# Gate sums of a recurrent stage by 64x64 blocks, and every second weight tile rounded by GpSimd

## The reference

```python
h = rmsnorm(x, norm_mix)
xr, gr, q, k, v, iq, ik, iw, ga, gb = split(h @ w_in)
# branch A, the recurrent one; D_RNN = 1024 channels in 16 blocks of 64
xc = causal_conv4(xr)
r = sigmoid(blockdiag(w_rg_a) @ xc + b_rg_a)       # 16 blocks of 64x64
i = sigmoid(blockdiag(w_rg_x) @ xc + b_rg_x)
log_a = 8 * r * log_sigmoid(lam)
a, u = exp(log_a), sqrt(-expm1(2 * log_a)) * (i * xc)
h_t = a_t * h_(t-1) + u_t                          # scan over the positions
branch_a = (h * gelu(gr)) @ w_rnn_out
# branch B: top-k by an indexer, then attention over the chosen keys with a position bias
branch_b = attend(q, k, v, iq, ik, iw) @ w_att_out
x += (sigmoid(ga) * branch_a + sigmoid(gb) * branch_b) @ w_o
x += swiglu(rmsnorm(x))
x += sigmoid(rmsnorm(x) @ w_ple_gate) * (p @ w_ple_proj)
y = rmsnorm(x)
```

## Time and profile before

| | us |
|---|---|
| median of 3 runs | 1044.59 (1043.33 to 1045.3) |
| the profiled execution, its own time | 1042.96 |
| its span in the profile | 1041.2 |
| PE busy | 1009.8 (97% of the span) |
| PEld (weight loads, beside PE) | 964.6 (93%) |
| DVE busy | 493.9 (47%) |
| ACT busy | 418.6 (40%) |
| POOL busy | 445.4 (43%) |

### The profile page before, as it was taken

How to read it: one execution, slowest core, us unless ns; L and a number is a source line. 1 busy time by engine, 2 the same in 40 slices (tenths; PEclk the granted TensorE clock), 3 DMA queues, 4 the chain that set the end, 5 groups by cost and what they waited for, 6 DMA issues and landing times.

```text
span 1041.2 us, 19261 instructions
## 1 busy us (share of the span) xinstructions
PE 1009.8 (97%) x7845; PEld 964.6 (93%) x7845; DVE 493.9 (47%) x769; ACT 418.6 (40%) x707; POOL 445.4 (43%) x301
## 2 busy tenths in 40 slices
PE   6999999999979999999999999999999999999997
PEld 4986998799978999899999999999999999999996
DVE  5127899588992534324364343333001333334474
ACT  5325234698983444323334322222112222233543
POOL 2424431367784444534542543343344334244530
PEclk9999999999999999999999999999999999999998
DMA  6733276452330443043253432322333322222502
GB/s 187 208 63 87 72 197 186 130 162 62 82 82 26 102 102 82 21 124 83 65 178 87 133 91 86 96 61 77 91 97 104 100 81 65 65 80 73 144 1 86
DMA packets 168751, 101.98 MB, mean 98 GB/s; under 512 B 12626, under 2 KB 160754, under 8 KB 168418
## 3 DMA queue, kind: packets, MB, share of 16 engines
q1 hardware_dynamic: 168674, 100.91, 34.4%
HBM read 93.26 MB, written 7.63 MB: 97 GB/s over the span
## 4 chain that ended last, share of the span: by engine, by line
PE 91%; DVE 4%; ACT 2%; DMA 1%; issue 1%; SPq 0%; POOL 0%; ACTq 0%; DVEq 0%; POOLq 0%
PE psD L1805 81%; PE psX L1753 2%; PE psX L2071 1%; PE held L1753 1%; PE psX L2000 1%; PE held L2095 1%; PE psX L1887 1%; DVE xn L1113 0%; DMA wraw<-in_w_in 0%; ACT whi L624 0%; DMA xtok<-in_x_prompt 0%; PE held L1957 0%; PE held L2014 0%; DVE xc L1170 0%; DVE hs L1351 0%
## 5 line engine op out<-in xcount | busy, mean ns | idle before, releaser
L1597 POOL TENSOR_TENSOR wlo<-wraw,whi 128x1024 fp32r<-128x1024 f32 (+3 forms) x216 | 389.7, 1817 | 548.0 <-ACT whi L624 543.0
L1805 PE MATMUL psD<-h_hi,whi 128*128 128x272 f32 (+1 forms) x1616 | 344.1, 294 | 0.5 <-POOL wlo L1597 0.5
L1805 PE MATMUL psD<-h_hi,wlo 128*128 128x272 f32 (+1 forms) x1616 | 335.9, 289 | 0.0
L1805 PE MATMUL psD<-h_lo,whi 128*128 128x272 f32 (+1 forms) x1616 | 335.2, 289 | 0.0
L1805 PEld LDWEIGHTS psD<-h_hi,whi 128*128 128x128 f32 (+1 forms) x1616 | 255.8, 189 | 11.8 <-issue 9.3
L1805 PEld LDWEIGHTS psD<-h_lo,whi 128*128 128x128 f32 (+1 forms) x1616 | 255.3, 189 | 0.0
L1805 PEld LDWEIGHTS psD<-h_hi,wlo 128*128 128x128 f32 (+1 forms) x1616 | 253.8, 189 | 0.0
L624 ACT CAST whi<-wraw 128x1024 fp32r<-128x1024 f32 (+4 forms) x165 | 154.9, 939 | 243.9 <-PE psD L1805 224.4
L1805 PE MATMUL psD<-act_hi,whi 128*128 128x272 f32 x672 | 140.8, 291 | 0.0
L1805 PE MATMUL psD<-act_hi,wlo 128*128 128x272 f32 x672 | 139.1, 288 | 0.0
L1805 PE MATMUL psD<-act_lo,whi 128*128 128x272 f32 x672 | 138.6, 288 | 0.0
(11 more groups left out here) (264 smaller groups left out, 986.2 us busy)
## 6 DMA issues: line engine op xcount, KB each, us to landing
wraw<-in_w_in SPq DMA_DIRECT2D x48, 512.0 KB, 4.6
wraw<-in_w_ffn_gate SPq DMA_DIRECT2D x22, 512.0 KB, 3.8
wraw<-in_w_ffn_up SPq DMA_DIRECT2D x22, 512.0 KB, 3.8
wraw<-in_w_ffn_down SPq DMA_DIRECT2D x16, 384.0 KB, 3.4
wraw<-in_w_ffn_down SPq DMA_DIRECT2D x16, 320.0 KB, 3.1
kpg<-in_cache_k SPq DMA_DIRECT2D x16, 256.0 KB, 3.1
wraw<-in_w_rnn_out SPq DMA_DIRECT2D x8, 512.0 KB, 4.9
wraw<-in_w_o SPq DMA_DIRECT2D x8, 512.0 KB, 6.4
```

The source lines that it names most:

```text
L1597: ins = g_.tensor_tensor(wlo[:, s, r0:r1, 0:cc], wraw[:, s, r0:r1, 0:cc], whi[:, s, r0:r1, 0:cc].bitcast(F32), ALU.subtract)
L1805: ins = te.matmul(psD[0:cc, b0 + half, 0:HT], w[:, s, c, 0:cc], m[:, k0 + c, HT * half:HT * (half + 1)], start=(part == 0 and c == 0 and w ...
```

## The change

It has two parts. **Gate sums by blocks:** the two matmuls of 128x128 of a call become four of 64x64, one for each quadrant of the array. For the first half of the columns (k = 0) the two blocks write their own partitions; for the second half (k = 1) they are crossed: block 0 writes partitions 64 to 127 and block 1 partitions 0 to 63. Both banks are asked for ahead of all four. ACT reads the crossed half with two instructions of 64 partitions that bring the rows back to their place, with a crossed copy of the biases (`crossed`, two small copies made once). **Rounding on GpSimd:** of the units 21 to 34, the seven even ones from 22 on are rounded by POOL in four pieces, ahead of their subtraction, and no longer by ACT. ACT waits, before it rounds the next unit, until POOL has rounded the one before it (`w_hi`).

```diff
+        def rounded_on_pool(n):
+            return isinstance(n, int) and U["xr"] + RING <= n < U["ga"] + 2 and n % 2 == 0
...
             def round_weights(n, it=0):
                 if n >= len(UNITS):
                     return
+                if rounded_on_pool(n):
+                    return
+                if rounded_on_pool(n - 1):
+                    act.wait_ge(w_hi, n)
...
             def gates(c, which):
-                    for k in range(2):
-                        job = ("gate", c, g, k)
-                        got_job(act, job)
-                        read_job(sc.activation(dst[:, EH * k:EH * (k + 1)], bank(job)[:, 0:EH], ACT.Tanh, scale=0.5,
-                                               bias=lru[:, 4 + g, c:c + 1]), job)
+                    job = ("gate", c, g, 0)
+                    got_job(act, job)
+                    read_job(sc.activation(dst[:, 0:EH], bank(job)[:, 0:EH], ACT.Tanh, scale=0.5,
+                                           bias=lru[:, 4 + g, c:c + 1]), job)
+                    job = ("gate", c, g, 1)
+                    got_job(act, job)
+                    for i, j in ((0, HD), (HD, 0)):
+                        ins = sc.activation(dst[i:i + HD, EH:EO], bank(job)[j:j + HD, 0:EH], ACT.Tanh, scale=0.5,
+                                            bias=crossed[j:j + HD, g, c:c + 1])
+                    read_job(ins, job)
...
+            act.wait_ge(lru_v, 1)
+            sc.copy(crossed[HD:P, :, :], lru[0:HD, 4:6, :])
+            link(sc.copy(crossed[0:HD, :, :], lru[HD:P, 4:6, :]))
             for c in range(DC):
                 gates(c, 0)
...
             def lower_weights(n, it=0):
                 s = n % RING
+                if rounded_on_pool(n):
+                    pool.wait_ge(w_loaded[s], 16 * (n // RING + 1))
+                    pool.wait_ge(w_used, n - RING + 1)
+                    for k in range(4):
+                        r0, r1 = rc * k // 4, rc * (k + 1) // 4
+                        ins = g_.tensor_copy(whi[:, s, r0:r1, 0:cc], wraw[:, s, r0:r1, 0:cc])
+                    ins.then_inc(w_hi, 1)
                 pool.wait_ge(w_hi, n + 1 + 4 * it)
...
             def gate_sums(c, g):
+                b = [start_job(("gate", c, g, k)) for k in range(2)]
+                if g == 0:
+                    pe.wait_ge(xc_ok, c + 1)
+                    if c == 0:
+                        pe.wait_ge(bd_in, 64)
                 for k in range(2):
-                    b = start_job(("gate", c, g, k))
-                    if g == 0 and k == 0:
-                        pe.wait_ge(xc_ok, c + 1)
-                        if c == 0:
-                            pe.wait_ge(bd_in, 64)
-                    end_job(te.matmul(b[:, 0:EH], bd[:, c, g, :], xc[c % 2][:, EH * k:EH * (k + 1)],
-                                      start=True, stop=True))
+                    for h in range(2):
+                        i, j = HD * h, HD * (h ^ k)
+                        ins = te.matmul(b[k][j:j + HD, 0:EH], bd[i:i + HD, c, g, i:i + HD],
+                                        xc[c % 2][i:i + HD, EH * k:EH * (k + 1)], start=True, stop=True,
+                                        tile_position=(i, j))
+                    end_job(ins)
```

More of the change, by code:

```diff
@@ L219, in hybrid_decoder_step @@
     sstat = place("sstat", [P, 8])
+    crossed = place("crossed", [P, 2, DC])
     top8 = place("top8", [P, 8])
```

## The result

| | before | after |
|---|---|---|
| median | 1043.96 us (4 runs, 1043.2 to 1045.3) | 1053.88 us (4 runs, 1051.83 to 1056.28) |
| ratio, 95% interval | | 1.0093 (1.0075 to 1.0112) |
| the profiled execution, its own time | 1042.96 | 1052.0 |
| its span | 1041.2 | 1050.3 |

The forecast was + 5.7 us, 1050.3; the time came at + 9.9, inside the range (1045.8 to 1055.0), in the direction foretold, and 3.6 above the predicted time. One of the eleven executions of a later kernel (the kernel before with the output's lower part in four pieces) took 1968.41 us; it counts in that kernel's median, 1044.00, which would be 1043.96 without it, and not in its ratio.

What follows compares the result with a forecast made beforehand. PE's turn (13.94 us) and the ACT-DVE loop (13.60) were nearly tied; the change would let the loop decide. 0.9 + 0.1 - 0.1 + 3.8 + 1.0 = + 5.7 on 1044.59 gave 1050.3 us, range 1045.8 to 1055.0.

Steps and rivals of the forecast that it cites:

- The bound: Recurrent stage from chunk 3: PE's turn 13.94 us, loop over ACT and DVE 13.60, nearly tied; with the change the loop decides.
- PE, 0.88 a call: Gate sums on PE: the four quadrants run together, 0.88 us a call against 0.96, 1.3 us off PE's list.
- the rival that rested on it: Gate sums on PE: quadrants don't run together, 2.32 us a call, about + 21 us, 1065; chance 0.06.
- ACT, + 0.87 a chunk: ACT between first tanh and square root: one more tanh step of 0.44 us per call, 0.87 a chunk, in the loop.
- GpSimd's pieces, 0.4 us each: Rounding pieces on POOL, four a chunk: about 0.4 us each uncovered, at most 1.09; POOL's list 12.9 us, which holds.
- the first rival: DVE's taps: GpSimd's earlier subtraction frees them, 3.43 to 2.4 us; total + 0.2, 1044.8, not slower; chance 0.17.
- POOL and DVE, + 0.3 a turn: POOL's rounding pieces and subtraction beside DVE: between - 1.0 and + 2.3 us a chunk, taken as + 0.3.
- Chunk 0 to 1, + 0.9: Second gate sum waits until ACT has read both halves of the first: + 0.9 us on PE's path.
- Chunk 1 to 2, + 0.1: Turn from chunk 1 to 2: loop looser, PE's turn 13.78 us, DVE busy for 10.21; + 0.1 us.
- The four turns, + 3.8: Turns from chunk 3 to 7: each 14.9 us instead of 13.94, together + 3.8 us.
- The end, + 1.0: From chunk 7's gate sum to DVE's last step: ACT's 0.87 and 0.10 us more, + 1.0; PE waits above 6 us.
- No clock cost: PE's half clock behind the end wait, at 311.5 to 315 us, is paid already; nothing added.

Runs made afterwards that it cites:

- PE's side alone: Changed kernel with each crossed half read by one 128-partition tanh (values wrong) and rounding back on ACT; 1044.28 us, ratio 0.9999.
- blocks alone: Changed kernel with the rounding on GpSimd undone, ACT rounding all units; 1050.79 us, ratio 1.0057.
- one read: Changed kernel with ACT reading each crossed half by one instruction of 128 partitions, values not the reference's; 1044.14 us, ratio 1.0004.
- split reads: Kernel before, with ACT reading each gate's second half by two instructions of 64 partitions, nothing crossed; 1048.69 us, ratio 1.0039.
- rounding alone: Changed kernel with full-array gate sums and their reads as before, only GpSimd's rounding kept; 1047.23 us, ratio 1.0032.
- The runs with four pieces: GpSimd's 544-column subtraction for the output's lower part cut in four: in the changed kernel 1050.05 us, in the kernel with only GpSimd's rounding 1043.49.
- the run with the seven added matmuls: Changed kernel with seven matmuls of 272 columns, results overwritten, ahead of each wait for DVE's taps from chunk 1 on; 1053.47 us, ratio 1.0089.

## Why the prediction was right, and where it was short

The length of the stage in the profiles, from chunk 0's first gate sum to the end of the end wait, splits the change into parts:

| part | from | us |
|---|---|---|
| quadrants | PE's side alone less before: 117.14 - 118.05 | - 0.9 |
| third tanh | blocks alone less PE's side alone: 123.71 - 117.14 | + 6.6 |
| third tanh | changed less one read: 127.60 - 120.93 | + 6.7 |
| third tanh | split reads less before: 121.99 - 118.05 | + 3.9 |
| GpSimd's rounding | changed less blocks alone: 127.60 - 123.71 | + 3.9 |
| GpSimd's rounding | one read less PE's side alone: 120.93 - 117.14 | + 3.8 |
| GpSimd's rounding | rounding alone less before: 121.30 - 118.05 | + 3.3 |

The steps - 0.9, + 6.6 and + 3.9 follow one another from the kernel before to the changed one, so they give its + 9.55 by their making; what supports them is that other pairs give about the same. The third tanh is the exception: 3.9 us in the kernel before, 6.6 behind the quadrants. Of the 2.6 between, 1.5 are the half clock in chunk 0 of the blocks' profile (18.48 against 16.95), behind a wait of 1.78 that the kernel with split reads does not have, and 0.9 are what the quadrants had saved on PE, which is worth nothing once the loop decides (turns of 14.45 with them, 14.50 without). Of the 6.7 about 1.5 are the half clock in the turn of 16.63. So the clock is a part of what the third tanh costs, by the waits that it makes.

The stage's length is not all of the time. One read and PE's side alone differ by 3.8 us in the stage and not in the median (1044.14 and 1044.28), for 727.1 us lie behind the stage of the first and 730.9 behind that of the second. What GpSimd's rounding costs in the median is 3.1 on top of the blocks and 3.5 alone, but nothing in this last pair, where the half clock comes to lie ahead of the end wait.

Step by step:

- **The bound.** "PE's turn (13.94) and the loop over ACT and DVE (13.60) are nearly tied", so that the loop would decide: right. PE waits for the taps 1.34 to 2.09 us ahead of the first sums of chunks 2 and 4 to 7 (forecast 0.5 to 1.2, from chunk 4 on), and 0.25 ahead of chunk 3's.
- **PE, 0.88 a call.** Measured 0.84. The quadrants ran together. In the changed kernel the eight records of the sum at 226.16 start within 0.31 us, the first passes of all four quadrants within 0.02, although both row tiles write each of the two banks. The Trainium skill ("TensorEngine Tiling (Array Packing)", section "Restrictions and Gotchas") says that different row tiles cannot access the same PSUM bank at once; this trace does not bear it out for four quadrants over two banks, and the rival that rested on it is out.
- **ACT, + 0.87 a chunk.** This is one of the two mis-sized terms: + 1.25 (8.31 against 7.06). The step was taken as half of the pair's 0.87; the two instructions of 64 partitions take 0.50 to 0.53 each, and a sum 1.53 where it took 0.92. "Worth nothing" for the roundings taken off ACT: right, the idle time ahead of the first tanh grew from 0.73 to 1.59.
- **GpSimd's pieces, 0.4 us each.** 0.41. POOL did not become the bound (at most 13.55 busy of a turn). The taps did come free as the first rival had it, from 3.43 to 2.50 in some chunks and 2.98 in others, but for chunk 6 (3.49), where `y_lower` lies beside them.
- **POOL and DVE, + 0.3 a turn.** The other mis-sized term, and the one with a mechanism that was not seen: not the added rounding pieces, but `y_lower`, a subtraction that was there before and stands where it stood on POOL's list, moved in time from behind the taps to beside L1355. By itself L1355 lost 1.04 us. With the taps' gain DVE's part came to 5.87 in some chunks and 6.62 in others, + 0.06 and + 0.81 against 5.81. Against the 5.21 of the blocks alone it is + 0.66 and + 1.41: ACT's longer part had moved DVE out of POOL's way, and the rounding put it back. The runs with four pieces (- 3.8 and - 3.7 us) show that the length of this one instruction is about all that the move to GpSimd costs (3.1 and 3.5).
- **Chunk 0 to 1, + 0.9.** + 0.92 in the profile, by the wait foretold for the second gate sum. "0.1" was added for the read; what was left out is that the clock can fall behind it.
- **Chunk 1 to 2, + 0.1.** + 1.19: the step that failed. It was argued from DVE's busy time of 10.21, but the loop there is ACT's 7.06 and DVE's 5.21, and with 8.31 and 5.87 it is above PE's list as in every other chunk. The loop had been followed in one chunk only.
- **Chunk 2 to 3, - 0.1.** - 0.13.
- **The four turns, + 3.8.** + 7.0: 15.12, 15.88, 16.63 and 15.14 less 4 x 13.95. The forecast's signs had turns of 14.5 to 15.3. In the turn of 16.63 the clock fell; in the run with the seven added matmuls, whose clock stays up, it is 15.00. With 15.12 in its place the four are + 5.5, by the two terms above, and the clock's share is + 1.5.
- **The end, + 1.0.** + 0.58: ACT's part is 1.24 longer, and DVE gives half of it back (for chunk 7 L1352 takes 0.46 where L1335 took 0.84, and L1355 0.73 where L1338 took 1.15). PE's wait at the end fell to 2.14, against the forecast of above 6, since PE met one more wait (1.59 for ACT's tanh, L834) and worked at half clock in between.
- **No clock cost.** Wrong within the stage. PE of the changed kernel in order of time, behind the wait of 2.09:

```profile
274.32 0.66 PE L1829 MATMUL psD<-h_hi,wlo 128*128 128x272 f32 x2
274.78 0.66 PE L1829 MATMUL psD<-h_hi,whi 128*128 128x272 f32 x2
275.23 0.66 PE L1829 MATMUL psD<-h_lo,whi 128*128 128x272 f32 x2
```

A pair's step is 0.45 instead of 0.25 up to 277.5, with the granted clock at the lower level, 1.2 of 2.4 GHz. The half unit takes 5.4 us instead of 3.85, so the second gate sum comes 1.5 us late. ACT waits 0.42 for it, its part is 8.83 instead of 8.32, and DVE starts late enough for `y_lower` (284.16 to 286.03) to lie beside two of its instructions:

```profile
283.67 1.14 DVE L1355 SCALAR_TENSOR_TENSOR sq<-dec,sq 128x568 f32<-128x568 f32 x1
284.73 1.91 DVE L1358 SCALAR_TENSOR_TENSOR ig<-ig,xc 128x568 f32<-128x568 f32 x1
```

DVE's part is 6.85. With the clock up, in the run with the seven added matmuls, the same chunk has 8.30 and 5.84. So about 1.5 us of the turn of 16.63 come from the clock, one third through ACT and two thirds through DVE.

So the direction, the engine that waits and whom it waits for were right. In the stage the forecast was short by 3.9 us: 1.1 in chunk 1's turn, 1.7 in the four turns by the tanh's step and `y_lower`, and 1.5 there by the clock, less 0.4 too much at the end. That the time still fell within the range is owed to its width: the forecast's own bound for DVE, + 1.1 a turn, made room for what it had not seen.

What stays open: how much of the median's + 9.9 is the clock in the stage. The profiled execution of the changed kernel (1052.0) has 1.5 us of it in chunk 5 and none in chunk 0; its others reach to 1056.28, and may have a half clock there, but they have no profile. Added matmuls in chunk 0 were not tried. And the 193 us ahead of the stage differ by up to 2.6 us between profiles of kernels that are alike there, so the 1.4 of the changed one cannot be put down to the change.

## What to carry to other kernels

Before an engine's instruction is split, ask what the split costs on the engine that reads the result: here quadrants saved TensorE 0.12 us a call and cost ScalarE 0.61. When work is moved onto an engine, list what stands behind it in that engine's order and what each will newly lie beside; the instruction that hurt was not one of the added ones, and four pieces in its place took nearly all of the cost away. Follow the loop in every chunk that differs, not in one.

## What the runs showed of the hardware

- Four 64 x 64 matmuls on the four quadrants, with two row tiles in each of two PSUM banks, start their first passes within 0.02 us and cost 0.84 us a call for two halves of two passes, against 0.96 for the whole array.
- A tanh of 284 columns takes as long over 64 partitions as over 128 (494 and 498 ns), and three in a row, two of them halves, take 1.53 where two whole ones take 0.92 (1.38 to 1.42 where the halves stay in their own partitions).
- A DVE instruction of 568 columns takes 0.73 alone, 1.77 beside one GpSimd subtraction of 544 columns, and 0.89 beside four of 136, though these take POOL 3.52 us instead of 1.58 and the next DVE instruction beside them takes 1.02 instead of 0.74.
- Behind PE's wait of 2.09 us in one turn the granted clock fell to the lower level; behind waits of 1.34 to 1.38 in other turns it did not, and behind a wait of 1.78 in chunk 0 it fell in four profiles of five. Near the stage's end it fell behind waits of 1.58 to 1.60 in all five profiles that have one, and with split reads behind one of 1.03, so the length of the last wait alone does not tell whether it falls. 36 matmuls without use in place of a 5.34 us wait brought 1.7 us.
